# A later place for branch B's layer normalisation, and for the residual of the second output tile, in a one-core hybrid RWKV step

## The chip, the cores and the metric

The kernel runs on one core of a Trainium2 chip. The metric is the time on the device in microseconds (us), the median of several runs. The engines are PE (TensorE, matrix products), DVE (VectorE), ACT (ScalarE), POOL (GpSimd) and SP, whose queue issues all transfers here. PEld is the loading of weights into TensorE.

## The reference

One layer, applied to 128 prompt tokens and to 1024 latent tokens. The normalised input `h` is projected once, and three branches read the result. Only what bears on the change is shown:

```
h = rms_norm(x, g_pre) * (1 + scale) + shift
za, zb, zc, gc = split(h @ w_in)
# branch B: width-31 depthwise convolution, LayerNorm over 256 channels, gates
u = conv_b(u1 * sigmoid(u2)) + conv_b_bias
mu = mean(u, -1);  var = mean(square(u - mu), -1)
u = (u - mu) * rsqrt(var + LN_EPS) * ln_b_g + ln_b_b
yb = silu(u) * silu(gb)
# branch C: token shift of zc, bidirectional scan, group norm, gate
zc = zc + mu_shift * (0.5 * (previous + next) - zc)
out = concatenate([ya, yb, yc], -1) @ w_out
x = x + gate * rms_norm(out, g_post)
```

## The kernel before

Channels lie on the 128 partitions, and the 1158 columns (`W`) hold the prompt and latent tokens with a few empty columns between. Five instruction streams are written by hand; each engine executes its own in the written order, and semaphores tie them together. There are three stages, with a barrier between them.

**Stage one, the projection.** PE goes through 32 tiles of 128 output channels (`for j, b in ...`, L667), numbered `j`. Every tile has three blocks `b` of 386 columns, and each block is 24 matmuls (L681 to L683: 8 slices of the input, three products of rounded halves and rests each). Two sets of three PSUM banks take turns, so that tile `j` may begin once tile `j-2` has been read (L676). Tiles 0 to 17 feed the branches and gates; `MIX0` is 18, and tiles 18 to 31 are the `mix` tiles of branch C. For a `mix` tile ACT copies the banks twice (L580 scaled by 1-mu, L581 into `raw`, which has two buffers; the semaphore `s_raw` counts these and is what releases PE), POOL adds left and right neighbours into the single buffer `nsum` (L482), and DVE adds this to the tile (L912). At every second tile ACT also rounds the next piece of weights (L515), and POOL subtracts it from the unrounded one (L470).

DVE computes branch B's convolution in pieces along tiles 6 to 17 (L829; its last tap raises `s_cv`). Then comes the layer normalisation, in three column thirds `n`. PE sums the means (L644, L645) into bank 6; DVE subtracts them (L853, `s_lx`); ACT squares (L547, `s_lq`); PE sums the squares (L652, L653) into bank 7; ACT takes the root (L549, `s_ls`); DVE inverts it (L856) and multiplies (L857). At the end DVE scales (L860), ACT takes a tanh (L552), and four DVE instructions apply both gates (L864, L866, `s_yb`). In PE's stream the four steps of this stand behind the blocks (18, 0), (18, 1), (18, 2) and (19, 0): step 0 is the first mean, steps 1 and 2 are the next mean and the squares of the third before it, step 3 the last squares. In ACT's and DVE's streams the whole normalisation is one piece behind tile 17, ahead of what tile 18 asks of them. The root goes to `raw[:, 0]`.

**Stage two** is the bidirectional scan in chunks of 64 tokens. The diff does not touch it.

**Stage three, the output.** Branch C's result is normalised by groups in three column blocks (`statistics`: sums on PE at L1723, L1727 and L1734, centring on DVE at L1905 and L1908, squares on ACT at L1837; `spreads`: L1747). Nine output tiles of 128 tokens are multiplied (`products`, L1780 to L1782: 48 matmuls each of 512 columns) into two pairs of banks. `finish(i)` on DVE scales such a tile by its inverse deviation and the gate (L1930, L1932, `s_og`) and adds the residual `x`, which a transfer brings into one of three slots (L1937, `s_or`); SP then stores it. SP issues the residual's loads of tiles 1 and 2 when three output tiles have been multiplied (L1704, `s_o` of 3). PE's order is

```
spreads(1); output(2); statistics(2); output(3); spreads(2); output(4) ... output(8)
```

and DVE's for the third block (`b == 2`) is `finish(1)`, four times `centre`, `finish(2)`, `invert(2)`, and the rest.

Of the kernel before, what the change touches and what calls it, by code (L numbers as in the profile page):

```python
# [30 lines left out]
P = 128  # L31
# [7 lines left out]
NB = 3  # L39
# [64 lines left out]
def hybrid_step_kernel(nc, x_prompt, x_sample, c, state_rwkv, c_ctx, ada_w, ada_b, g_pre, g_post, w_in,  # L104
# [3 lines left out]
    with ctx:  # L108
# [225 lines left out]
        with nc.Block() as block:  # L334
# [150 lines left out]
            def _(act):  # L485
# [57 lines left out]
                def layer_norm():  # L543
                    for n in range(NB):
                        cut = slice(n * NC, (n + 1) * NC)
                        act.wait_ge(s_lx, n + 1)
                        act.activation(T[:, 2:4, cut], T[:, 0:2, cut], ACT.Square).then_inc(s_lq, 1)  # L547
                        act.wait_ge(s_lv, n + 1)
                        act.activation(raw[:, 0, cut], ps[:, 7, 0:NC], ACT.Sqrt, bias=epst[:, 1:2]).then_inc(s_ls, 1)  # L549
                    for g in range(2):  # L550
                        act.wait_ge(s_lr, g + 1)
                        act.activation(T[:, 2 + g, :], T[:, g, :], ACT.Tanh, scale=0.5).then_inc(s_lt, 1)  # L552

                round_weights(1)
                for j, kind in enumerate(TILES):
                    h, z = j % 2, zbanks(j)
                    i = j - TILES.index(kind)
                    if kind in ("u2", "gb", "ga", "gc", "xa", "mix"):
                        act.wait_ge(s_z, j + 1)
                    if kind == "u2":  # L560
                        act.activation(as3(T[:, h, :]), z, ACT.Tanh, scale=0.5).then_inc(s_th, 1)
                    elif kind == "gb":
                        if h == 0:
                            act.wait_ge(s_sg, 32)
                        act.activation(as3(T[:, 6 + h, :]), z, ACT.Tanh, scale=0.5).then_inc(s_th, 1)
                    elif kind == "xa":
                        act.activation(as3(xa[:, h, :]), z, ACT.Copy).then_inc(s_xa, 1)
                    elif kind == "ga":
                        act.activation(as3(xa[:, 2 + h, :]), z, ACT.Tanh, scale=0.5).then_inc(s_th, 1)
                    elif kind == "mix":  # L570
                        if i < 2:
                            act.wait_ge(s_ya, i + 1)
                        if i == 4:
                            act.wait_ge(s_yb, 2)
                        if i == 6:
                            act.wait_ge(s_sb, 16)
                        if i >= 2:
                            act.wait_ge(s_sum, i - 1)

                        act.activation(as3(dest(i)), z, ACT.Copy, scale=omu[:, i:i + 1])  # L580
                        act.activation(as3(raw[:, i % 2, :]), z, ACT.Copy).then_inc(s_raw, 1)  # L581
                    elif kind == "gc":
                        act.activation(as3(T[:, 4 + i, :]), z, ACT.Tanh, scale=0.5).then_inc(s_th, 1)
                    if h and (j + 3) // 2 < len(PIECES):
                        round_weights((j + 3) // 2)
                    if j == MIX0 - 1:
                        layer_norm()
                    if MIX0 + 5 <= j <= MIX0 + 8:
                        kk_norm(j - MIX0 - 5)
                    if j == MIX0 + 13:  # L590
                        act.wait_ge(s_mix, 13)
                        act.activation(lwT, lwT, ACT.Tanh).then_inc(s_lwt, 1)

            @block.tensor
            def _(pe):
# [71 lines left out]
                for j, b in [(j, b) for b in range(NB) for j in range(2)] + [(j, b) for j in range(2, len(TILES)) for b in range(NB)]:  # L667
                    p = j // 2
                    cut = slice(P * (j % 2), P * (j % 2) + P)
                    w_hi = w_round[:, p % 2, :].rearrange("p (k n) -> p k n", k=KT)  # L670
                    w_lo = w_rest[:, slot_of("z", p), :].rearrange("p (k n) -> p k n", k=KT)
                    if j % 2 == 0 and b == 0:
                        pe.wait_ge(s_wh, p + 1)
                        pe.wait_ge(s_wo1, p + 1)
                    if j >= 2 and b == 0:
                        pe.wait_ge(*read_by(j - 2))  # L676
                    o, cols_b = ps[:, NB * (j % 2) + b, 0:NC], slice(NC * b, NC * (b + 1))
                    for k in range(KT):
                        if j == 0:
                            pe.wait_ge(s_hs, KT * b + k + 1)  # L680
                        pe.matmul(o, w_hi[:, k, cut], hi_of_h[:, k, cols_b], start=(k == 0), stop=False)  # L681
                        pe.matmul(o, w_hi[:, k, cut], lo_of_h[k][:, cols_b], start=False, stop=False)  # L682
                        last = pe.matmul(o, w_lo[:, k, cut], hi_of_h[:, k, cols_b], start=False, stop=(k == KT - 1))  # L683
                    if b == NB - 1:
                        last.then_inc(s_z, 1)
                    if j == MIX0 or (j == MIX0 + 1 and b == 0):
                        layer_norm(NB * (j - MIX0) + b)
                    if MIX0 + 6 <= j <= MIX0 + 9 and b == 0:
                        kk_norm(j - MIX0 - 6)
                    if b < NB - 1:  # L690
                        continue
                    g = p - GATE_AFTER
                    if j % 2 and 0 <= g < GATES:
                        pe.wait_ge(s_wl[slot_of("gate", g)], 16 * (turn_of("gate", g) + 1))
                        if g == 0:
                            pe.wait_ge(s_pclear, 2)
                        for k in (2 * g, 2 * g + 1):
                            for b in range(4):
                                at = D_MODEL * (k % 2) + 256 * b
                                last = pe.matmul(ps[32 * b:32 * b + 2, 6, 0:256], mods[:, k, :], ring[:, slot_of("gate", g), at:at + 256],  # L700
                                                 start=(k == 0), stop=(k == KT - 1))
                        last.then_inc(s_gu, 1)
# [10 lines left out]
            def _(dve):  # L713
                n_dve = [0]

                def link(ins):
                    n_dve[0] += 1
                    ins.then_inc(s_dve, 1)
                    dve.wait_ge(s_dve, n_dve[0])
# [127 lines left out]
                                                      in1=og[:, :, lo:hi], op0=ALU.mult, op1=ALU.add))  # L847

                def layer_norm():
                    for n in range(NB):  # L850
                        cut = slice(n * NC, (n + 1) * NC)
                        dve.wait_ge(s_lm, n + 1)
                        dve.tensor_tensor(T[:, 0:2, cut], T[:, 4:6, cut],  # L853
                                          ps[:, 6, 0:NC].unsqueeze(1).to_broadcast([P, 2, NC]), ALU.subtract).then_inc(s_lx, 1)
                        dve.wait_ge(s_ls, n + 1)
                        link(dve.reciprocal(raw[:, 0, cut], raw[:, 0, cut]))  # L856
                        link(dve.tensor_tensor(T[:, 0:2, cut], T[:, 0:2, cut],  # L857
                                               raw[:, 0, cut].unsqueeze(1).to_broadcast([P, 2, NC]), ALU.mult))
                    for g in range(2):
                        dve.tensor_scalar(T[:, g, :], T[:, g, :], col("ln_b_g", g), col("ln_b_b", g),  # L860
                                          ALU.mult, ALU.add).then_inc(s_lr, 1)
# [14 lines left out]
                for j, kind in enumerate(TILES):  # L876
# [42 lines left out]
                        dve.scalar_tensor_tensor(out=as3(T[:, 4 + i, :]), in0=as3(T[:, 4 + i, :]), scalar=1.0, in1=z,  # L919
                                                 op0=ALU.add, op1=ALU.mult).then_inc(s_gc, 1)  # L920
                    conv_some(taps_after.get(j, 0))
                    if j == MIX0 - 1:
                        layer_norm()

        assert sems1 == list(range(sems1[0], sems1[0] + len(sems1)))
# [751 lines left out]
        with nc.Block() as block:  # L1677
# [223 lines left out]
            def _(dve):  # L1901
# [23 lines left out]
                                             op0=ALU.mult, op1=ALU.mult).then_inc(f_yc, 1)  # L1925

                def finish(i):
                    b, slot = 2 * (i % 2), i % XO
                    dve.wait_ge(s_os, i + 1)
                    dve.reciprocal(rs2[:, i:i + 1], ss2[:, i:i + 1]).then_inc(f_dve, 1)  # L1930
                    dve.wait_ge(f_dve, i + 1)
                    dve.scalar_tensor_tensor(out=gout[:, i % 2, :], in0=ps[:, b:b + 2, :].rearrange("p b n -> p (b n)"),  # L1932
                                             scalar=rs2[:, i:i + 1], in1=gg[:, min(i, 1), :],
                                             op0=ALU.mult, op1=ALU.mult).then_inc(s_og, 1)
                    dve.wait_ge(s_og, i + 1)
                    dve.wait_ge(s_xr[slot], 16 * (i // XO + 1))
                    dve.tensor_tensor(xr[:, slot, :], xr[:, slot, :], gout[:, i % 2, :], ALU.add).then_inc(s_or, 1)  # L1937
# [6 lines left out]
                for b in range(NB):  # L1944
                    group = range(4 * b, 4 * b + 4)
                    if b == 2:
                        finish(1)
                    for n in group:
                        centre(n)
                    if b == 1:  # L1950
                        dve.wait_ge(s_gg, 16)
                    if b:
# [43 lines left out]
```

## Time and profile before

| what | value |
|---|---|
| median of 3 runs | 1121.65 us (1118.37 to 1122.81) |
| the profiled execution's own time | 1118.77 us |
| its span, first to last instruction | 1117.1 us |
| PE busy | 1013.8 us, 91% |
| DVE, ACT, POOL busy | 643.6, 427.3, 404.3 us |
| mean granted TensorE clock | 0.961 of full |

The time of a run contains the span and some 1.7 us around it. Stage one lasts to about 507 us of the span, stage three begins at 957 us. A timeline row gives start and duration in us, the engine, the line, the operation with its output and input, and in brackets how long the engine was idle before it and what ended that.

### The profile page before, as it was taken

How to read it: one execution, taken by the hardware profiler on the slowest of the kernel's cores; microseconds unless marked ns; L12 is line 12 of the kernel's file. 1: busy time of each engine (PE TensorE's matmuls, PEld its weight loads, DVE VectorE, ACT ScalarE, POOL GpSimd, SP SyncE). 2: the span in 40 equal slices, each digit the busy share in tenths (PEclk: the TensorE clock that was granted, in tenths of full speed). 3: DMA queues.
4: the chain of work that ended last, by engine and by line, in shares of the span. 5: the costliest groups of instructions: out<-in, count | busy, mean ns of one | idle time of the engine just before them, and what ended most of it. 6: DMA issues, size and time to landing. Idle time of an engine off the chain costs nothing. (4 is left out here: it accounts for less than half of the span.)

```text
span 1117.1 us, 32049 instructions
## 1 busy us (share of the span) xinstructions
PE 1013.8 (91%) x14407; PEld 910.3 (81%) x14407; DVE 643.6 (58%) x954; ACT 427.3 (38%) x708; POOL 404.3 (36%) x372
## 2 busy tenths in 40 slices
PE   5699999999889999993699999999999998698997
PEld 3399999999779888982699988999899987365685
DVE  5440079584463312254678878888888884455532
ACT  5351101101242333222355655565566653543311
POOL 7111222111104321312446555566666663402110
PEclk9799999999899999996699999999999999899999
DMA  9613322111112110000000000000000000721231
GB/s 359 247 39 108 129 76 77 38 38 39 38 48 102 50 38 1 1 1 10 1 4 4 4 14 4 4 4 4 4 4 4 4 4 4 272 106 58 94 113 57
DMA packets 30036, 61.46 MB, mean 55 GB/s; under 512 B 3352, under 2 KB 21444, under 8 KB 28748
## 3 DMA queue, kind: packets, MB, share of 16 engines
q1 hardware_dynamic: 29900, 59.42, 15.0%
q8 instruction: 114, 1.87, 0.7%
q14 instruction: 22, 0.18, 0.1%
HBM read 49.68 MB, written 9.73 MB: 53 GB/s over the span
## 5 line engine op out<-in xcount | busy, mean ns | idle before, releaser
L681 PE MATMUL ps<-input_rounded,weights_rounded 128*128 128x386 f32 x768 | 264.8, 345 | 4.2 <-DVE input_rest L788 3.1
L683 PE MATMUL ps<-input_rounded,weights_rest 128*128 128x386 f32 x768 | 260.3, 339 | 0.0
L682 PE MATMUL ps<-input_rest,weights_rounded 128*128 128x386 f32 x768 | 260.3, 339 | 0.0
L1402 POOL TENSOR_TENSOR arena<-arena,lvl 128x512 f32<-128x512 f32 x108 | 138.8, 1300 | 77.0 <-ACT arena L1319 46.3
L681 PEld LDWEIGHTS ps<-input_rounded,weights_rounded 128*128 128x128 f32 x768 | 145.3, 189 | 11.9 <-issue 9.3
L470 POOL TENSOR_TENSOR weights_rest<-arena,weights_rounded 128x2048 fp32r<-128x2048 f32 x16 | 74.6, 4662 | 210.7 <-ACT weights_rounded L515 210.7
L682 PEld LDWEIGHTS ps<-input_rest,weights_rounded 128*128 128x128 f32 x768 | 145.4, 189 | 0.9 <-issue 0.6
L683 PEld LDWEIGHTS ps<-input_rounded,weights_rest 128*128 128x128 f32 x768 | 145.5, 189 | 0.0
L1118 PE MATMUL ps<-arena 64*64 64x64 f32 x2880 | 106.0, 224 | 18.2 <-issue 14.7
L1118 PEld LDWEIGHTS ps<-arena 64*64 64x64 f32 x2880 | 94.5, 137 | 23.8 <-issue 17.0
L1128 PE MATMUL ps<-arena 64*64 64x64 f32 x2880 | 104.9, 223 | 4.5 <-DVE arena L1528 4.1
L1325 ACT ACTIVATE arena<-ps 128x512 f32<-128x512 f32 x90 | 53.8, 597 | 130.2 <-DVE arena L1532 124.7
L912 DVE SCALAR_TENSOR_TENSOR zc<-arena,hmu,zc 128x1156 f32<-128x1156 f32 x14 | 41.4, 2957 | 107.1 <-POOL arena L482 107.1
L1128 PEld LDWEIGHTS ps<-arena 64*64 64x64 f32 x2880 | 92.9, 137 | 10.2 <-DVE arena L1528 6.1
L482 POOL TENSOR_TENSOR arena<-arena 128x1156 f32<-128x1156 f32 x14 | 30.3, 2164 | 154.2 <-ACT arena L581 151.5
L829 DVE SCALAR_TENSOR_TENSOR zc<-zc,cb 128x113 f32<-128x113 f32 (+14 forms) x120 | 77.4, 687 | 1.8
L1528 DVE TENSOR_TENSOR arena<-eyes,ps 128x512 f32<-128x512 f32 x90 | 61.4, 682 | 23.2 <-PE ps L1118 22.1
L515 ACT ACTIVATE weights_rounded<-arena 128x2048 fp32r<-128x2048 f32 x16 | 30.7, 1917 | 97.9 <-DMA arena<-in_w_in 52.0
L1532 DVE STREAM_TRANSPOSE arena<-ps 128x512 f32<-128x512 f32 x72 | 51.2, 711 | 25.5 <-PE ps L1128 25.4
L580 ACT ACTIVATE zc<-ps,omu 128x1158 f32<-128x1158 f32 x14 | 17.2, 1228 | 110.8 <-PE ps L683 110.8
L1507 DVE TENSOR_TENSOR arena<-ps,tri 128x512 f32<-128x512 f32 x72 | 46.4, 686 | 16.7 <-PE ps L1098 16.7
L1098 PE MATMUL ps<-arena 64*128 64x128 f32 x576 | 44.2, 297 | 11.1 <-DVE arena L1499 11.1
(247 smaller groups left out, 1711.2 us busy)
## 6 DMA issues: line engine op xcount, KB each, us to landing
arena<-in_w_in SPq DMA_DIRECT2D x16, 1024.0 KB, 5.2
arena<-in_ada_w SPq DMA_DIRECT2D x7, 1024.0 KB, 5.3
mix_scratch<-zc SPq DMA_DIRECT2D x4, 1158.0 KB, 9.6
out<-arena SPq DMA_DIRECT2D x9, 512.0 KB, 2.6
zc<-in_x_sample SPq DMA_DIRECT2D x4, 1024.0 KB, 8.8
hT<-in_ada_w SPq DMA_DIRECT2D x4, 1024.0 KB, 11.9
zc<-in_w_out SPq DMA_DIRECT2D x4, 1024.0 KB, 13.9
arena<-in_x_sample SPq DMA_DIRECT2D x8, 512.0 KB, 3.5
```

Source lines behind the costliest of these rows:

```text
L470: pool.tensor_tensor(w_rest[:, at, :], ring[:, at, :], w_round[:, p % 2, :].bitcast(F32), ALU.subtract).then_inc(s_wo1, 1)
L681: pe.matmul(o, w_hi[:, k, cut], hi_of_h[:, k, cols_b], start=(k == 0), stop=False)
L682: pe.matmul(o, w_hi[:, k, cut], lo_of_h[k][:, cols_b], start=False, stop=False)
L683: last = pe.matmul(o, w_lo[:, k, cut], hi_of_h[:, k, cols_b], start=False, stop=(k == KT - 1))
L829: done = dve.scalar_tensor_tensor(out=o[:, a:b], in0=x[:, a + off * step:b + off * step], scalar=w, in1=o[:, a:b], op0=ALU.mult, op1=ALU.add)
L1118: last = pe.matmul(bank(0)[r, h, :], Um[l % 3][r, h, :], X[n % 2][r, h, :], start=True, stop=True)
L1128: last = pe.matmul(bank(1)[r, h, :], PX[r, h, :], Y[n % 2][r, h, :], start=True, stop=True)
L1325: act.activation(Y[n % 2], bank(1), ACT.Copy).then_inc(q_Y, 1)
L1402: pool.tensor_tensor(Um[l % 3], UT, lvl[:, l, :].unsqueeze(1).to_broadcast([P, 2 * PAIRS, C]), ALU.mult).then_inc(q_um[l], 1)
L1507: dve.tensor_tensor(GM[n % 2][:, d, h:h + PAIRS].rearrange("p a s c -> p a (s c)"), ps[:, 4 + 2 * d + g, :].rearrange("p (a k) -> p a k", ...
L1528: dve.tensor_tensor(PX, eye8(), bank(0), ALU.subtract).then_inc(q_F, 1)
L1532: dve.transpose(X[n % 2], bank(1)).then_inc(q_X, 1)
```

## The change

Three things are changed.

1. Branch B's normalisation stands one tile later in all three streams: behind tile 18's work on ACT and DVE, and in PE's stream behind the blocks (19, 0), (19, 1), (19, 2) and (20, 0). The root goes to `kn`, which is unused at that time, and no longer to `raw[:, 0]`, which tile 18 now fills before.
2. On DVE the subtraction of the mean of a third stands ahead of the inversion and product of the third before it: centre 0, centre 1, divide 0, centre 2, divide 1, divide 2.
3. `finish(1)` is cut in two. `scale_output(1)` stays ahead of the four `centre` of the third block, and `add_residual(1)`, which waits for the loaded residual, stands behind them.

```diff
@@ ACT @@
-                        act.activation(raw[:, 0, cut], ps[:, 7, 0:NC], ACT.Sqrt, bias=epst[:, 1:2]).then_inc(s_ls, 1)
+                        act.activation(kn[:, cut], ps[:, 7, 0:NC], ACT.Sqrt, bias=epst[:, 1:2]).then_inc(s_ls, 1)
...
-                    if j == MIX0 - 1:
+                    if j == MIX0:
                         layer_norm()
@@ PE @@
-                    if j == MIX0 or (j == MIX0 + 1 and b == 0):
-                        layer_norm(NB * (j - MIX0) + b)
+                    if j == MIX0 + 1 or (j == MIX0 + 2 and b == 0):
+                        layer_norm(NB * (j - MIX0 - 1) + b)
@@ DVE @@
                 def layer_norm():
-                    for n in range(NB):
+                    def centre(n):
                         cut = slice(n * NC, (n + 1) * NC)
                         dve.wait_ge(s_lm, n + 1)
                         dve.tensor_tensor(T[:, 0:2, cut], T[:, 4:6, cut],
                                           ps[:, 6, 0:NC].unsqueeze(1).to_broadcast([P, 2, NC]), ALU.subtract).then_inc(s_lx, 1)
+
+                    def divide(n):
+                        cut = slice(n * NC, (n + 1) * NC)
                         dve.wait_ge(s_ls, n + 1)
-                        link(dve.reciprocal(raw[:, 0, cut], raw[:, 0, cut]))
+                        link(dve.reciprocal(kn[:, cut], kn[:, cut]))
                         link(dve.tensor_tensor(T[:, 0:2, cut], T[:, 0:2, cut],
-                                               raw[:, 0, cut].unsqueeze(1).to_broadcast([P, 2, NC]), ALU.mult))
+                                               kn[:, cut].unsqueeze(1).to_broadcast([P, 2, NC]), ALU.mult))
+
+                    centre(0)
+                    centre(1)
+                    divide(0)
+                    centre(2)
+                    divide(1)
+                    divide(2)
...
-                    if j == MIX0 - 1:
+                    if j == MIX0:
                         layer_norm()
@@ stage three, DVE @@
                 def finish(i):
-                    b, slot = 2 * (i % 2), i % XO
+                    scale_output(i)
+                    add_residual(i)
+
+                def scale_output(i):
+                    b = 2 * (i % 2)
                     dve.wait_ge(s_os, i + 1)
...
+
+                def add_residual(i):
+                    slot = i % XO
                     dve.wait_ge(s_og, i + 1)
                     dve.wait_ge(s_xr[slot], 16 * (i // XO + 1))
...
                     if b == 2:
-                        finish(1)
+                        scale_output(1)
                     for n in group:
                         centre(n)
+                    if b == 2:
+                        add_residual(1)
```

## Rows read from the trace of the kernel before

**Rows 1.** The page: the span, and the granted TensorE clock in 40 slices.

```profile
span 1117.1 us, 32049 instructions
...
PEclk9799999999899999996699999999999999899999
```

**Rows 2.** The waits from 283.9 to 343: who waited, total us, times, longest.

```profile
PE ps L644 <- DVE zc L829: 4.6, 1, 4.6
...
PE ps L681 <- ACT arena L581: 0.9, 1, 0.9
```

**Rows 3.** ACT's timeline from 275 to 385: its tile work and the last root.

```profile
283.95 1.14 ACT L569 ACTIVATE zc<-ps 128x1158 f32<-128x1158 f32 x1 [11.54 <-PE ps L683]
...
320.38 0.59 ACT L549 ACTIVATE arena<-ps,epst 128x386 f32<-128x386 f32 x1 [3.01 <-PE ps L653]
...
328.76 1.13 ACT L581 ACTIVATE arena<-ps 128x1158 f32<-128x1158 f32 x1
...
342.98 1.23 ACT L580 ACTIVATE zc<-ps,omu 128x1158 f32<-128x1158 f32 x1 [9.15 <-PE ps L683]
...
355.66 1.23 ACT L580 ACTIVATE zc<-ps,omu 128x1158 f32<-128x1158 f32 x1 [10.42 <-PE ps L683]
```

**Rows 4.** PE's timeline in the normalisation.

```profile
300.39 0.81 PE L644 MATMUL ps<-zc,arena 128*128 128x386 f32 x2
301.04 0.81 PE L645 MATMUL ps<-zc,arena 128*128 128x386 f32 x2
...
308.41 0.92 PE L644 MATMUL ps<-zc,arena 128*128 128x386 f32 x2 [1.02 <-DVE zc L853]
...
317.42 1.63 PE L652 MATMUL ps<-zc,arena 128*128 128x386 f32 x2 [1.91 <-ACT zc L547]
```

**Rows 5.** DVE's timeline from 275 to 385.

```profile
287.91 4.77 DVE L829 SCALAR_TENSOR_TENSOR zc<-zc,cb 128x113 f32<-128x113 f32 x2
...
307.40 0.96 DVE L853 TENSOR_TENSOR zc<-zc,ps 128x772 f32<-128x772 f32 x1
311.93 2.57 DVE L856 RECIPROCAL arena<-arena 128x386 f32<-128x386 f32 x1 [3.57 <-ACT arena L549]
...
333.88 1.42 DVE L912 SCALAR_TENSOR_TENSOR zc<-arena,hmu,zc 128x1156 f32<-128x1156 f32 x1
337.52 5.75 DVE L912 SCALAR_TENSOR_TENSOR zc<-arena,hmu,zc 128x1156 f32<-128x1156 f32 x1 [2.23 <-POOL arena L482]
```

**Rows 6.** POOL's timeline from 275 to 385.

```profile
335.38 2.12 POOL L482 TENSOR_TENSOR arena<-arena 128x1156 f32<-128x1156 f32 x1 [2.64 <-DVE zc L912]
337.45 4.61 POOL L470 TENSOR_TENSOR weights_rest<-arena,weights_rounded 128x2048 fp32r<-128x2048 f32 x1
```

**Rows 7.** Stretches: us, PE, PEld, DVE, ACT, POOL busy, granted clock, DMA share, GB/s.

```profile
283.90:343.00 59.10, 50.66 (x243) 44.79 (x242) 36.53 (x21) 18.15 (x18) 14.83 (x4) 0.91 0.17 56
1024.80:1039.90 15.10, 10.64 (x26) 3.66 (x25) 5.51 (x9) 4.57 (x9) 0.00 (x0) 0.89 0.65 201
```

**Rows 8.** The chain that ended last, from 1003 to 1042: start, us, what.

```profile
1004.77 0.44 PE ps L1780
...
1024.99 3.88 DMA arena<-in_x_sample
1028.97 1.22 DVE arena L1937
...
1039.84 0.43 PE ps L1780
```

**Rows 9.** PE's timeline from 992 to 1052: how two passes of the statistics begin.

```profile
995.45 0.81 PE L1723 MATMUL ps<-hT,heads 128*128 128x384 f32 x2
...
1024.80 0.81 PE L1723 MATMUL ps<-hT,heads 128*128 128x386 f32 x2
```

**Rows 10.** DVE's timeline around the third block's centring.

```profile
1022.05 1.28 DVE L1932 SCALAR_TENSOR_TENSOR arena<-ps,small,arena 128x1024 f32<-128x1024 f32 x1
...
1040.32 0.16 DVE L1930 RECIPROCAL small<-small 128x1 f32<-128x1 f32 x1 [1.28 <-ACT small L1830]
```

## The prediction

> **What bounds the kernel now.** I read the page first: the span is 1117.1 us [rows 1], and by the table PE is busy for 91% of it, so only what PE waits for, or loses to its clock, can be won. The page's line of granted clock shows where it is not full: in the slices around 280 to 307 us, in 503 to 558, and near the start of stage three [rows 1]. Then I asked who waited for whom in the stretch that part 1 and 2 of the change touch, 283.9 (the end of tile 17) to 343.0 (the end of tile 20) [rows 3]. PE waits there four times: 4.6 us for the convolution's last tap, 0.9 us for ACT's second copy of tile 18 [rows 2], 1.02 us for the subtraction of the second mean and 1.91 us for the last squares [rows 4], 8.4 us in all. ACT and DVE are not short of time there, 18 and 37 us busy out of 59 [rows 7]. They wait too, because each third of the normalisation is a round trip over three engines with only one block of matmuls to cover it. In stage three the chain of what ended last has one stretch that isn't PE: the load of a residual, 1024.99 to 1028.9, and the addition behind it, to 1030.2 [rows 8].
>
> **Parts 1 and 2, the normalisation.** First what PE's work there takes at full clock. A mix tile lasts 355.66 - 342.98 = 12.68 us, a block a third of it, 4.23 [rows 3]. One matmul call of the normalisation takes 301.04 - 300.39 = 0.65 us [rows 4], and there are twelve, 7.8. Three tiles and these make 38.0 + 7.8 = 45.8 us. The stretch lasted 342.98 - 283.9 = 59.1. The surplus of 13.3 is 8.4 of waits and 4.9 of low clock and release times. The low clock shows as 1.63 us for a pair that takes 0.81 otherwise, right behind the wait of 1.91, and not behind the wait of 1.02 (0.92) [rows 4]; the mean granted clock is 0.91 [rows 7].
>
> Now the new order, which I laid out step by step with the durations of before. The convolution ends at 287.91 + 4.77 = 292.7 [rows 5]; PE asks for it only behind block (19, 0), at 283.9 + 12.7 + 4.2 = 300.8. So the wait of 4.6 is gone, with 8 us to spare. New in front of the normalisation is tile 18's own work: ACT copies it from 296.6 to 299.0, POOL adds neighbours in 2.12 [rows 6] to 301.2, DVE adds in 1.42 [rows 5] to 302.6. PE's first mean is ready at about 302.2, so DVE is 0.4 late, and the subtraction (0.96 [rows 5]) ends at 303.6. PE wants that at 306.3, behind (19, 1): covered by 2.7. PE's step 1 gives the second mean at 307.6 and the first variance at 309.0. DVE subtracts at once (308.7, wanted at 313.1), which is what the new order on DVE is good for; the root ends at 309.7, ACT then squares the second third (0.85) to 310.6, wanted at 314.4. The inversion (2.57 [rows 5]) and product (0.96) run to 313.3, before the third mean at 314.5. Squares of the last third: 315.5 for the subtraction, 316.5 for ACT to have made the second root, 317.4; wanted at 320.0, behind (20, 0): covered by 2.6. So none of the three older waits inside the normalisation is left.
>
> The fourth changes its place. ACT can't read tile 19 before it has done both tanh, and PE can't begin tile 21 before tile 19 is read. In before ACT's last root begins at 320.38, and the first tile's second copy ends at 329.89 [rows 3]: 9.5 us, with the inversion, product, scaling and both tanh between. PE's last variance is now ready at 321.4, so `s_raw` reaches 2 at 330.9, and with the 0.4 us that PE took to resume in before (342.98 - 12.68 = 330.3, against 329.89), tile 21 begins at 331.3. Its wait is 331.3 - 329.7 = 1.6. In before it began at 343.0. **The gain is 11.7 us.**
>
> What is late next: DVE's four gate instructions end at about 334.9, beside POOL's work as in before. DVE's addition for tile 19 is slowed by POOL's subtraction of weights (5.75 instead of 1.42, beside 4.61 of POOL [rows 5, 6]) and ends near 340; POOL's sum and DVE's addition for tile 20 end at 343.5, ACT wants to copy tile 21 at 344.0. The lag is gone there. ACT rounds the weights of tile 22 at 331 to 333, POOL's rest is there by 338, and PE needs it at 344.0. SP's queue: the weight loads hang on PE's tiles and come earlier with them. The store of `yb` stands behind the load that tile 21 releases, at 344; `yb` is ready at 335. The root's other buffer costs nothing, being of the same size on the same engines. Nothing here adds an instruction.
>
> **Part 3, the residual.** DVE had scaled tile 1 by 1022.05 + 1.28 = 1023.3 [rows 10] and then stood still until the residual had landed; the load was only issued when PE had multiplied the third tile, at 1025.0 [rows 8]. The four `centre` were queued behind it, PE's statistics behind these. The same pass for the second block shows what it costs without such a wait: 995.45 to 1004.77, 9.32 us, against 1024.80 to 1039.84, 15.04 us [rows 8, 9]. Part of the difference is low clock behind PE's idle time (0.89 granted [rows 7]). With the addition behind the centring, DVE and ACT are idle at 1024.8 just as they were at 995.4. **The gain is 5.7 us.** The bounds are 0, if something unseen is last instead, and 5.7.
>
> The moved addition takes 1.22 us [rows 8]. It comes at 1033.4, when the residual has long landed, and fits the 1.28 us in which DVE waited for ACT's deviation of tile 2 [rows 10]. If that cover were gone it would delay `invert(2)`, whose result PE wants only after a whole output tile, 11 us. The store of tile 1 is issued some 2 us later, and behind it in SP's queue the load of tile 4's residual, which is not needed for another 20 us.
>
> **The sum.** 11.7 + 5.7 = 17.4 us. From the profiled execution, 1118.77, that gives 1101.4; from the median, 1121.65, it gives 1104.2. The profiled one lies near the fast end of the runs, so I take the mean of all four executions, 1120.4, and forecast **1103.0 us**.
>
> **The rivals.**
>
> *The new wait costs clock.* The wait of 1.6 lies between one of 1.02 that left the clock full and one of 1.91 that halved it [rows 4]. Half clock for some 4 us costs about 2; the surplus of before, 4.9 for two such places, says the same. Time: 1105. The Trainium skill (TensorE: Matmul & The Clock Gate, Part 1: The HAM clock gate) adds that the moments of judgement run free of the kernel, so the same kernel can differ from run to run. By that rule the price would be paid in some runs only, and the stretch of 503 to 558 at low clock could come out a little longer or shorter too; the forecast stays between 1101 and 1107 either way.
>
> *One part only.* (a) Tile 18's work ahead of the normalisation delays it, and PE's waits come back. For it speaks that DVE's addition can take 5.75 beside POOL [rows 5]. Against it: POOL's next large instruction hangs on ACT's rounding, which now comes after the normalisation. If 4.3 us were added at one place, the covers of 2.7 would let 1.6 through, three times with low clock some 7: 1110; if all of it, 1114.7. (b) The statistics wait for something else that was hidden: 1103.0 + 5.7 = 1108.7. Against it, the pass of 9.32 us in the same code.
>
> *No change.* The waits are attributed to the wrong releaser and stay: 1120.4. The two parts have different places, so both would have to fail.
>
> *Slower.* PE stays at half clock after the new wait. A dense tile then takes 12.7 us more; with two tiles, 25 us are lost against 17.4 gained, 1128. It decides from 1.4 tiles on. For it: 503 to 558, where the clock stayed low for long [rows 1]. Against it: that is the sparse start of the scan, and nowhere between tiles 0 and 31 did it stay low beyond a few us.
>
> **How the numbers follow.** Forecast, with full clock 0.60; with the lost clock 0.20; one part only 0.12 (half of that within reach of 1109); no change 0.05; slower 0.03. The first two and the nearer part-only cases hold over 0.8. The range goes down to 1098.5: fastest run 1118.4 less 17.4 is 1101, and less low clock at the scan's start may give another 2 or 3. Up it goes to 1109: the slowest run, 1122.8, less 17.4, plus 2 is 1107.4, and the case with part 1 and 2 alone 1108.7. About 0.5%, 5.6 us, is what a measurement of this kernel can tell from no change. Faster by more: 0.92, as even the one-part cases mostly give 5.7 or more; within: 0.05; slower: 0.03.
>
> **What the profile after would show.** Tile 21's first copy by ACT comes 11.7 us sooner, near 344 instead of 355.66; no PE wait at L644 or L652 over 0.5 us; one at L681 of 1.2 to 1.6 for L581; the statistics' second pass lasts 9.3 us and the DMA is off the chain; the span is near 1099.7. Wrong I would be if PE waits in the normalisation for DVE's subtraction or ACT's squares, if tile 22 or 23 waits for POOL's or DVE's backlog, or if the clock behind the new wait stays low.

## The result, and the profile after

The changed kernel takes 1102.05 us (median of 4 runs, 1101.02 to 1105.55), against 1121.11 us in the same session for the kernel before. The ratio is 0.9844, with a 95% interval of 0.9822 to 0.9866. (A ratio here and below is the recorded estimate, not the quotient of the two medians, which is 0.9830; the one stands for 17.5 us, the other for 19.1.) A second series of 5 runs on another occasion gave 1101.87 us and the same ratio, 0.9844 (0.9820 to 0.9868), against 17 runs of the kernel before. The forecast was 1103.0. Behind line 854, numbers of source lines in the changed kernel are higher: L853 is the subtraction in both; L856 and L857 became L859 and L860, the two gate lines L864 and L866 became L874 and L876, L912 became L922, L1905 became L1915, L1723 became L1733, L1780 became L1790, L1930 became L1944, L1937 became L1954.

The page after, to set beside [rows 1]: span, busy shares, granted clock.

```profile
span 1100.7 us, 32049 instructions
...
PE 1007.3 (92%) x14407; PEld 907.2 (82%) x14407; DVE 644.0 (59%) x954; ACT 427.1 (39%) x708; POOL 406.1 (37%) x372
...
PEclk9799999999999999995699999999999999989999
```

The number of instructions is the same, and the engines' busy times moved little: DVE by 0.4 us, ACT by 0.2, POOL by 1.8, PE by 6.5, which goes with the higher mean clock (0.967 granted, against 0.961). The dip of the clock around 280 to 307 us is gone; the one at the scan's start stayed, and so did the one in which stage three begins, one slice further on. The dip in the third block's statistics is too short for these slices: from 1032 to 1037 us the granted clock was 0.77 in the kernel before, while in the changed kernel every stretch of 5 us from 972 to 1047 has 1.00.

The waits of the changed kernel from 283 to 345, to set beside [rows 2]:

```profile
DVE zc L853 <- PE ps L645: 5.7, 2, 4.3
...
PE ps L681 <- ACT arena L581: 1.2, 1, 1.2
```

In this stretch PE waits once, where it waited four times. The subtraction now waits for PE and not PE for the subtraction. PE's timeline in the changed kernel, to set beside [rows 4], shows the four steps:

```profile
300.85 0.81 PE L644 MATMUL ps<-zc,arena 128*128 128x386 f32 x2
...
306.36 0.81 PE L644 MATMUL ps<-zc,arena 128*128 128x386 f32 x2
...
313.20 0.81 PE L644 MATMUL ps<-zc,arena 128*128 128x386 f32 x2
...
320.02 0.81 PE L652 MATMUL ps<-zc,arena 128*128 128x386 f32 x2
...
331.14 0.44 PE L681 MATMUL ps<-input_rounded,weights_rounded 128*128 128x386 f32 x1 [1.22 <-ACT arena L581]
```

No bracket stands at the four steps, and each pair takes 0.81 us, at a granted clock of 1.00 all through the stretch. The prediction had them at 300.8, 306.3, 313.1 and 320.0, and tile 21's begin at 331.3. ACT in the changed kernel, to set beside [rows 3]:

```profile
284.13 1.14 ACT L569 ACTIVATE zc<-ps 128x1158 f32<-128x1158 f32 x1 [11.54 <-PE ps L683]
...
321.52 0.58 ACT L549 ACTIVATE arena<-ps,epst 128x386 f32<-128x386 f32 x1 [4.20 <-PE ps L653]
...
329.96 1.12 ACT L581 ACTIVATE arena<-ps 128x1158 f32<-128x1158 f32 x1
...
344.13 1.23 ACT L580 ACTIVATE zc<-ps,omu 128x1158 f32<-128x1158 f32 x1 [9.09 <-PE ps L683]
```

The last row is tile 21's copy, which stood at 355.66 in [rows 3]. And DVE, to set beside [rows 5]:

```profile
307.86 0.96 DVE L853 TENSOR_TENSOR zc<-zc,ps 128x772 f32<-128x772 f32 x1 [4.27 <-PE ps L645]
309.77 2.57 DVE L859 RECIPROCAL arena<-arena 128x386 f32<-128x386 f32 x1 [0.95 <-ACT arena L549]
...
335.09 5.79 DVE L922 SCALAR_TENSOR_TENSOR zc<-arena,hmu,zc 128x1156 f32<-128x1156 f32 x1
343.11 1.43 DVE L922 SCALAR_TENSOR_TENSOR zc<-arena,hmu,zc 128x1156 f32<-128x1156 f32 x1 [2.23 <-POOL arena L482]
```

The second subtraction is over before the first inversion begins. The addition that runs beside POOL's subtraction of weights takes 5.79 us, not 1.42, and ends at 340.9; the next ends at 344.5, and PE waits for neither.

In stage three the chain that ended last, in the changed kernel between 980 and 1030, goes over the centring and no longer over a transfer (compare [rows 8]):

```profile
1014.22 0.66 PE ps L1733 x2
1014.88 0.02 issue
1014.91 0.57 DVE hT L1915
...
1023.42 0.43 PE ps L1790
```

With 1014.06 as the pass's first matmul it lasts 9.36 us, where [rows 8, 9] gave 15.04. DVE's timeline of the changed kernel shows where the moved addition went:

```profile
1022.53 1.22 DVE L1954 TENSOR_TENSOR arena<-arena 128x1024 f32<-128x1024 f32 x1
1023.89 0.16 DVE L1944 RECIPROCAL small<-small 128x1 f32<-128x1 f32 x1
```

The second row has no bracket any more, while in [rows 10] DVE was idle for 1.28 us ahead of it. The addition filled that hole.

### The profile page after: what moved, and what is told of

Same layout as the page of the kernel before. It is cut to its first block and busy times, and to the rows that moved or that the text cites. A ratio compares the mean times of both kernels' runs of the same rounds, so it can differ in the third digit from the quotient of the medians.

```text
span 1100.7 us, 32049 instructions
## 1 busy us (share of the span) xinstructions
PE 1007.3 (92%) x14407; PEld 907.2 (82%) x14407; DVE 644.0 (59%) x954; ACT 427.1 (39%) x708; POOL 406.1 (37%) x372
## 5 line engine op out<-in xcount | busy, mean ns | idle before, releaser
L922 DVE SCALAR_TENSOR_TENSOR zc<-arena,hmu,zc 128x1156 f32<-128x1156 f32 x14 | 41.4, 2960 | 104.1 <-POOL arena L482 104.1
L1138 PEld LDWEIGHTS ps<-arena 64*64 64x64 f32 x2880 | 93.3, 137 | 10.7 <-DVE arena L1538 6.4
```

What stands on the lines that cost most here:

```text
L1138: last = pe.matmul(bank(1)[r, h, :], PX[r, h, :], Y[n % 2][r, h, :], start=True, stop=True)
```

## The experiments

To compare kernels I cut each profiled execution at marks that all have. *17 to 21* runs from ACT's first row behind tile 17 (283.95 in the kernel before) to PE's begin of tile 21. That begin is read as ACT's first copy of tile 21 less the 12.68 us of a dense tile: 344.13 - 12.68 - 284.13 = 47.32 in the changed kernel, 355.66 - 12.68 - 283.95 = 59.03 in the kernel before. *Pass two* is the third block's statistics. *Scan* runs from the transfer that fetches the scan's state to the first of stage three; no kernel here changes anything in it.

| kernel | 17 to 21 | pass two | scan | span | ratio to before (95%) |
|---|---|---|---|---|---|
| before | 59.03 | 15.04 | 449.55 | 1117.1 | |
| changed | 47.32 | 9.36 | 450.33 | 1100.7 | 0.9844 (0.9822 to 0.9866) |
| changed, again | 47.32 | 9.36 | 448.44 | 1098.3 | 0.9844 (0.9820 to 0.9868) |
| residual only | 57.15 | 9.36 | 453.59 | 1113.6 | 0.9946 (0.9928 to 0.9963) |
| normalisation only | 47.32 | 15.00 | 449.44 | 1104.6 | 0.9902 (0.9881 to 0.9923) |
| one tile later, old order | 50.71 | 15.04 | 449.73 | 1108.3 | 0.9926 (0.9906 to 0.9947) |
| old place, new order | 53.84 | 14.92 | 448.40 | 1110.7 | 0.9952 (0.9937 to 0.9967) |
| changed, copies before tanh | 45.84 | 9.36 | 453.14 | 1102.2 | 0.9811 (0.9789 to 0.9833) |
| root's buffer only | 59.04 | 15.37 | 453.43 | 1120.6 | 1.0012 (0.9996 to 1.0028) |
| PE one block later | 54.64 | 15.07 | 451.26 | 1114.4 | 0.9966 (0.9946 to 0.9986) |

The first two rows make up the profiled difference: 11.7 and 5.7 us gained, 0.8 lost in the scan, and 0.2 by which tile 17 ended later; 16.4 in all. The second series was expected to repeat 47.3 and 9.4 and to differ by up to 2 us at the scan's start; it gave 47.32 and 9.36, and its whole scan was 1.9 us shorter. In the four profiles with part 3 pass two took 9.36 us, in the six without it 14.92 to 15.37.

**The residual alone.** The kernel before, with this:

```diff
                     if b == 2:
-                        finish(1)
+                        scale_output(1)
                     for n in group:
                         centre(n)
+                    if b == 2:
+                        add_residual(1)
```

> The kernel before with the third part alone: the addition of the second output tile's residual behind the third block's centring. My account (the addition's wait for its load holds up PE's statistics): the second pass of the statistics falls from 15.04 us to 9.3, the load leaves the chain, the span falls by 5.7 us, the median by about 0.5%. Rival, part of the 15.04 is something else that the load only hid: the pass ends between 10 and 15 us. Rival, the first part's change made the gain in stage three too, by shifting it in time: no gain here. The normalisation stretch stays at 59 us in either.

Pass two took 9.36 us, the chain has no transfer in it between 1005 and 1045 us, and the ratio is 0.9946, 6.0 us. The account holds. The profiled span fell by 3.5 only, since that execution's scan was 4.0 us longer than in the kernel before. It also brought something I had not looked for: the stretch 17 to 21 took 57.15 us, where 59 was expected. PE's timeline of this kernel has the third of the old waits, as long as in [rows 4]:

```profile
299.89 0.81 PE L644 MATMUL ps<-zc,arena 128*128 128x386 f32 x2
...
316.91 0.92 PE L652 MATMUL ps<-zc,arena 128*128 128x386 f32 x2 [1.92 <-ACT zc L547]
```

The pair behind the wait takes 0.92 us, not 1.63: the clock stayed full, in the same code. From there to tile 21 this kernel needs 1.35 us less. The rest of the 1.9 us between 57.15 and 59.03 was gained earlier. The first row is PE's step 1; it comes 15.92 us behind ACT's row of tile 17 (283.97), in the kernel before 16.44. There the low clock around the first wait, that of 4.6 us, lasted longer. So both spells of low clock differ between two executions of the same code.

**The normalisation alone.** The changed kernel, with the diff above taken back.

> The changed kernel with finish(1) whole again: parts 1 and 2 alone. My account: tile 21 begins 11.6 us sooner than in the kernel before, the statistics' second pass takes 15 us again, the span falls by 10.7 to 11.7 us, depending on what the clock does at the start of the scan. Rival, the two parts overlap or feed each other: with the 5.7 of the other part the two do not add up to the 16.4 us of span that both together gave.

47.32 us again, 11.7 less than before, and the ratio is 0.9902. The span fell by 12.5, more than the 10.7 to 11.7 expected; 0.6 of it is that tile 17 ended earlier in this execution (283.38 against 283.95). PE's wait for the centring, which stands behind the residual's addition again, is back in PE's timeline of this kernel:

```profile
1018.19 1.31 PE L1733 MATMUL ps<-hT,heads 128*128 128x386 f32 x2 [4.35 <-DVE hT L1915]
```

The ratios of the two halves multiply to 0.9946 x 0.9902 = 0.9849, against 0.9844 measured for both. By the ratios the two add up.

**One tile later, DVE in the old order.** The normalisation-only kernel with

```diff
-                    centre(0)
-                    centre(1)
-                    divide(0)
-                    centre(2)
-                    divide(1)
-                    divide(2)
+                    for n in range(NB):
+                        centre(n)
+                        divide(n)
```

> Part 1 alone: the normalisation one tile later, but DVE in the old order, each third centred only after the division of the third before. My account: the wait for the convolution (4.6 us) is gone; the second subtraction ends at 314.3 where PE wants it at 313.1, the third's squares at 323.3 where PE wants them at 321.3, so waits of about 1.2 and 2.0 come back, the second with low clock behind it, and tile 21 begins near 335.5: about 7.5 us ahead of the kernel before, 4 behind both parts together. Rival, the order is worth nothing once the tile in between is there: tile 21 begins at 331.3 and the gain is 11.7.

The waits from 280 to 345 in this kernel:

```profile
PE ps L652 <- ACT zc L547: 1.9, 1, 1.9
PE ps L681 <- ACT arena L581: 1.1, 1, 1.1
PE ps L644 <- DVE zc L853: 1.0, 1, 1.0
```

The convolution's wait is gone, and the two waits of the round trip are back as forecast (1.0 and 1.9 us, forecast 1.2 and 2.0). Once the place is changed, the order is worth 50.71 - 47.32 = 3.4 us. I had said 4: I had counted low clock behind the wait of 1.9, and there was none here: the granted clock was 1.00 from 301 to 345 us.

**Old place, DVE in the new order.** The kernel before with only the lines for `centre` and `divide` of the diff, the root still in `raw[:, 0]`.

> Part 2 alone: DVE's new order at the old place, the root in the old buffer. My account: the convolution's wait of 4.6 us and the low clock behind it stay; the waits of 1.02 and 1.91 inside the normalisation go, and with them one spell of low clock; the wait for tile 18's copies grows from 0.9 to about 1.6. Tile 21 begins 4.9 us sooner than in the kernel before. Rival, the place alone matters: less than 1 us. If parts 1 and 2 were simply additive, this and the run with part 1 alone would sum to 11.7; I expect 12.4, so nearly that.

The waits from 280 to 345 in this kernel:

```profile
PE ps L644 <- DVE zc L829: 4.6, 1, 4.6
PE ps L681 <- ACT arena L581: 1.3, 1, 1.3
```

53.84, 5.2 us less than before, where I had said 4.9. The two inner waits are gone. Against the kernel before, the two single parts give 8.3 and 5.2 us, 13.5 together, more than the 11.7 of both. But each of them is also measured against the 1.9 us of low clock that the profiled execution of the kernel before had on top. Against the residual-only kernel, whose first stage is the same code without these 1.9 us, they give 6.4 and 3.3, and both together 9.8. So in the profiled executions place and order are additive, and the surplus is low clock counted twice. The ratios show a surplus too (8.3 and 5.4 us against 11.0 for both), but with intervals of some 2 us each way they settle nothing on it.

**The root's buffer alone.** The kernel before with `kn[:, cut]` for `raw[:, 0, cut]` at the root, the inversion and the product.

> The kernel before with nothing but the root's buffer changed, from the first half of raw to kn. My account: no effect, ratio 1.000 within what the runs can tell; the four waits of 4.6, 1.0, 1.9 and 0.9 us as before, give or take 0.3 where the clock differs. Rival: the buffer itself makes the inversion or the root faster or slower, by more than 0.1 us each.

Four waits of 4.6, 1.0, 1.9 and 0.6 us, 59.04 us, ratio 1.0012 (0.9996 to 1.0028), and each inversion takes 2.57 us as before, to 0.01. The buffer does nothing that these runs can tell. In PE's timeline the pair behind the wait of 1.92 takes 1.25 us here:

```profile
317.66 1.25 PE L652 MATMUL ps<-zc,arena 128*128 128x386 f32 x2 [1.92 <-ACT zc L547]
```

The clock fell here too, but only within this pair (the granted clock is 1.00 from 317 to 318 us and 0.56 from 318 to 319; in the kernel before it was 0.74 from 317 to 318 already). That made this spell 0.4 us cheaper than in the kernel before. The spell at the first wait was 0.4 us dearer: step 1 comes 16.85 us behind tile 17, against 16.44. That 59.04 and 59.03 agree is in part chance.

**PE one block later, ACT and DVE at the old place.** The kernel with DVE's new order, and

```diff
-                    if j == MIX0 or (j == MIX0 + 1 and b == 0):
-                        layer_norm(NB * (j - MIX0) + b)
+                    if 0 <= NB * (j - MIX0) + b - 1 <= NB:
+                        layer_norm(NB * (j - MIX0) + b - 1)
```

> DVE's new order, and PE's four steps one block later (behind the second and third block of tile 18 and the first two of tile 19), but ACT and DVE still take the whole normalisation ahead of what tile 18 asks of them. My account: the convolution's wait falls from 4.6 to some 0.3 us, but the copies of tile 18 now come 9.5 us behind the last root, near 322.8, while PE has finished tile 19 at 317.4: a wait of 5 to 6 us at L681 for L581 takes its place, with low clock behind it. Tile 21 begins 51.9 to 54 us behind the end of tile 17, 0 to 2 us better than 53.8 of the run with DVE's order alone, and 4.6 or more short of the changed kernel. Rival, PE's place is all that matters: 47.3 us.

PE's timeline in this kernel:

```profile
292.81 0.92 PE L644 MATMUL ps<-zc,arena 128*128 128x386 f32 x2 [0.48 <-DVE zc L829]
...
323.28 0.66 PE L681 MATMUL ps<-input_rounded,weights_rounded 128*128 128x386 f32 x1 [5.52 <-ACT arena L581]
```

The wait of 4.6 became 0.48, and a wait of 5.52 took its place, as the account says. I had the sum slightly wrong: 54.64, 0.8 worse than 53.84, where I expected 0 to 2 better. From PE's first matmul of tile 20 to its end by ACT's copies (323.28 to 338.56) it took 15.3 us. The same piece behind the short wait of the changed kernel took 13.0 (331.14 to 344.13), so low clock behind the long wait cost 2.3. That PE's place is all that matters is refuted: without moving tile 18's copies ahead of the normalisation, ACT's order turns the gain into another wait.

**Copies before tanh.** The changed kernel, with ACT's piece cut in two:

```diff
+                def layer_norm_tanh():
                     for g in range(2):
                         act.wait_ge(s_lr, g + 1)
                         act.activation(T[:, 2 + g, :], T[:, g, :], ACT.Tanh, scale=0.5).then_inc(s_lt, 1)
...
+                    if j == MIX0 + 1:
+                        layer_norm_tanh()
                     if h and (j + 3) // 2 < len(PIECES):
                         round_weights((j + 3) // 2)
```

> The changed kernel, but ACT copies tile 19 before it computes the two tanh of the normalisation and not behind them. My account: the last PE wait there (1.22 us) is ACT's order alone; the two copies (2.3 us) fit the 3.3 us in which ACT waits for DVE's scaling, so the wait vanishes, tile 21 begins at 329.7 where the changed kernel begins it at 331.3 (45.8 us behind the end of tile 17, not 47.3), and the time falls by 1.2 to 1.6 us, about 0.13%. Rival, POOL's sum of neighbours now runs beside DVE's product and scaling and slows them as the addition was slowed (5.75 for 1.42): the normalisation ends some 4 us later, yb with it, but PE would still not wait; only if tile 22 or 23 then waits for the backlog is the time the same or worse.

ACT's timeline in this kernel, where L582 and L583 are the copies, L554 is the tanh and L687 the last matmul of a block:

```profile
322.27 1.22 ACT L582 ACTIVATE zc<-ps,omu 128x1158 f32<-128x1158 f32 x1
323.38 1.14 ACT L583 ACTIVATE arena<-ps 128x1158 f32<-128x1158 f32 x1
...
328.55 2.24 ACT L554 ACTIVATE zc<-zc 128x1158 f32<-128x1158 f32 x2 [2.73 <-DVE zc L874]
...
342.92 1.23 ACT L582 ACTIVATE zc<-ps,omu 128x1158 f32<-128x1158 f32 x1 [8.18 <-PE ps L687]
```

PE has no wait left between 280 and 345, and tile 21 begins after 45.84 us: 1.5 earlier than in the changed kernel, to the tenth what three tiles and twelve calls take at full clock. The rival's mechanism is real too, as DVE's timeline shows (L864 is the product in this kernel, L880 the gates' last instruction, L926 the addition):

```profile
325.08 2.52 DVE L864 TENSOR_TENSOR zc<-zc,arena 128x772 f32<-128x772 f32 x1
...
333.85 5.67 DVE L880 SCALAR_TENSOR_TENSOR zc<-zc 128x1158 f32<-128x1158 f32 x1
339.43 1.41 DVE L926 SCALAR_TENSOR_TENSOR zc<-arena,hmu,zc 128x1156 f32<-128x1156 f32 x1
```

The product takes 2.52 instead of 0.96 beside POOL's sum, the last gate instruction 5.67 instead of 3.16 beside POOL's subtraction, and the normalisation ends 4 us later than in the changed kernel, counted from tile 17. PE waits for neither. The median is 1099.5 against 1101.87 for the changed kernel in the same group, ratios to before 0.9811 and 0.9844. The intervals overlap, so the runs alone don't settle so small a difference; the trace does for the wait. By the median it is the fastest kernel measured here.

## Why the prediction was right

**What bounds.** PE's waits, and low clock behind them, were the whole of it: with no wait left (copies before tanh) the stretch takes 45.84 us, and the prediction had 45.8 for the work alone. Both accounts hold part by part: the place alone removed the convolution's wait, the order alone the two inner ones, the residual alone the one in stage three.

**Parts 1 and 2.** Predicted 11.7 us, measured 59.03 - 47.32 = 11.7. Of the instants that were laid out, the convolution's slack, the subtraction 0.4 us late behind tile 18's addition, and PE's four steps came within 0.2 us. The new wait at tile 21 was 1.22 us by the trace; with the time to resume it cost 1.5 (47.32 against 45.84), where the text had 1.6.

**Part 3.** Predicted 5.7, measured 5.68. That the moved addition would be hidden in 1.28 us of idle time is shown by the missing bracket.

**The backlog.** The addition slowed to 5.79 us ended at 340.9 (said: near 340), the following one at 344.5 (said: 343.5), with no PE wait. POOL's subtraction of weights took 5.75 us there, not 4.61, and was done at 339.7 where the text had 338; PE needed its result at 344.0 only.

**The clock.** Here the account was wrong in one step, and the forecast held in part by luck. The text took the wait of 1.91 as one that lowers the clock. Four profiles have that wait in the same place of a round trip (1.91 to 1.92 us). The clock fell behind it in two of them (pairs of 1.63 and 1.25 us) and stayed full in the other two (0.92 and 0.92): it is a matter of the execution, and a wait of this length cost between nothing and 1.35 us of the stretch. The new wait of 1.22 cost no clock in any of the three profiles that have it. One of the prediction's rivals named the Trainium skill (TensorE: Matmul & The Clock Gate, Part 1: The HAM clock gate), by which the moments at which the clock is decided are not tied to the kernel; the four pairs above agree with that. So 1.9 of the 11.7 us are clock that another execution of the same first stage didn't lose there: against the residual-only profile parts 1 and 2 give 9.8. With 9.8 the sum would have given 1104.9, inside the range but further from what was measured. Which of the two most executions of the kernel before do isn't shown, since only profiled ones can be read.

**The sum.** 17.4 was forecast; the profiled spans differ by 16.4, the medians by 19.1 with four runs each, and by 17.4 (1119.26 against 1101.87) in the group with 17 and 5 runs. So close a hit is partly luck: the clock's 1.9 us and the scan's share could each have fallen otherwise. The term not in the sum is the scan, 0.8 us longer in the changed kernel's first profile and 1.1 shorter in its second.

**The rivals.** One part only, no change, and slower are out: each part was there alone and together. That tile 18's work would delay the normalisation did not happen: POOL's large subtraction began at 333.9 us, behind the normalisation, as argued.

## What to carry to other kernels

When three engines hand a small piece of work round in thirds, let each engine first do what the next engine waits for, and only then the long operation that nobody waits for yet. Begin the piece late enough that its first input is long there. Then check each in-order queue for what now stands behind the piece: moving PE's steps without moving ACT's turned a wait of 4.6 us into one of 5.5. A wait for a transfer belongs behind all work that doesn't need it.

## What the runs showed of the hardware

The scan is the same code in all ten profiles, yet it took from 448.4 to 453.6 us. Two places make most of this. One is its end. These are stretches at the same distance from stage three, the first of the kernel before, the second of the residual-only kernel (columns as in [rows 7]):

```profile
937.00:947.00 10.00, 6.70 (x198) 6.07 (x195) 4.76 (x8) 1.79 (x3) 2.27 (x2) 1.00 0.02 5
```

```profile
939.20:949.20 10.00, 7.49 (x152) 7.04 (x150) 3.47 (x6) 1.19 (x2) 0.26 (x1) 0.59 0.01 2
```

With PE about as busy the granted clock was 1.00 in one execution and 0.59 in the other, and the scan took 4.0 us more. The same dip is in two other profiles, those with the root's buffer and with the copies before tanh (0.60 and 0.58), whose scans took 453.43 and 453.14 us, and a shallower one in that with PE one block later (0.75, 451.26 us). Four us stand beside a spread of 5.8 over the 17 runs of the kernel before (1116.57 to 1122.38), and beside 1.5 that the last experiment wanted to measure. The runs show such steps in their times as well: of the six of the normalisation-only kernel four took 1106.3 to 1106.9 us, at a mean granted clock of 0.966, and two 1110.9 and 1111.0, at 0.961 and 0.960; that these two had the dip isn't shown, since they have no profile. What decides it isn't settled here; kernels with and without the change have it.

The other is its start, where PE leaves the low clock earlier or later. In the changed kernel's first profile:

```profile
543.40:548.40 5.00, 4.78 (x64) 4.47 (x66) 3.31 (x6) 1.78 (x3) 1.49 (x2) 0.50 0.00 0
548.40:553.40 5.00, 5.00 (x136) 4.72 (x134) 3.22 (x5) 2.95 (x7) 0.07 (x1) 0.93 0.02 3
```

In the kernel before, 11.6 us later on its own axis, the second of these stretches had clock 1.00. DVE's instructions of the scan ran 11.6 us ahead of the kernel before up to there, and 11.2 ahead behind it.
